# One weight split moved from the end of the attention loop to the end of the head projections

## The reference, cut to what matters

```
qkv = (h @ w_qkv).reshape(B, S, 3, N_DIL, N_HEADS, HEAD_DIM)      # layer A: 3 groups; layer B: 1 group
q, k = rope(rmsnorm(q)), rope(rmsnorm(k))
scores = q @ k.T * scale;  scores = where(mask, scores, -inf)
p = exp(scores - max);  o = p @ v / sum(p)
x = x + attn @ w_o;  x = x + conv_ffn(rmsnorm(x))
```

## Time and profile before

| what | value |
|---|---|
| median of 3 runs | 1137.72 us |
| lowest and highest | 1136.93 and 1138.73 us |
| time of the profiled execution | 1137.72 us |
| its span (first to last instruction) | 1135.9 us, so 1.8 us lie around it |
| mean granted clock of PE | 0.992 |
| attention of `half_a0` and `half_a1`, first transpose | at 452.2 and at 583.5 us |
| attention of `half_b0` and `half_b1`, first transpose | at 858.3 and at 908.3 us |

### The profile page before, as it was taken

The page is one execution under the profiler, slowest core; times in us unless marked ns, Lnnn a source line. Parts: engine busy times, 40 slices in busy tenths (PEclk is TensorE's granted clock), DMA queues, the critical chain, the costliest instruction groups (busy, mean ns, idle before and its releaser), DMA issues.

```text
span 1135.9 us, 19220 instructions
## 1 busy us (share of the span) xinstructions
PE 1115.0 (98%) x7046; PEld 974.4 (86%) x7046; DVE 790.6 (70%) x1439; ACT 641.0 (56%) x1086; POOL 13.3 (1%) x23
## 2 busy tenths in 40 slices
PE   9998899999999999999999999999999999999998
PEld 7876789989987888888888999999887779999997
DVE  5867656555557667477675787787885757877876
ACT  5465455454456556565564665555666556655554
POOL 0000100000000000000000000000000000000000
PEclk9998899999999999999999999999999999999999
DMA  9552145666646565055622466556552624665562
GB/s 322 164 181 75 56 131 186 186 186 190 190 136 199 172 188 164 20 188 165 203 95 92 133 195 211 185 170 200 168 174 87 196 89 142 186 207 192 160 207 103
DMA packets 117037, 184.34 MB, mean 162 GB/s; under 512 B 6640, under 2 KB 70384, under 8 KB 116720
## 3 DMA queue, kind: packets, MB, share of 16 engines
q1 hardware_dynamic: 116688, 183.23, 51.1%
q10 hardware_dynamic: 288, 0.29, 0.1%
HBM read 182.45 MB, written 1.05 MB: 162 GB/s over the span
## 4 chain that ended last, share of the span: by engine, by line
PE 89%; DVE 4%; ACT 3%; issue 2%; DMA 1%; SPq 0%; DVEq 0%; ACTq 0%
PE ps L679 10%; PE ps L655 10%; PE ps L681 10%; PE ps L680 10%; PE ps L657 10%; PE ps L656 10%; PE ps L739 5%; PE ps L738 5%; PE ps L740 5%; PE ps L815 2%; PE ps L832 2%; PE ps L797 2%; PE ps L858 1%; ACT w_hi L1132 1%; DVE w_lo L1649 1%
## 5 line engine op out<-in xcount | busy, mean ns | idle before, releaser
L1649 DVE TENSOR_TENSOR w_lo<-w_stage,w_hi 128x1024 fp32r<-128x1024 f32 x336 | 403.6, 1221 | 191.8 <-ACT w_hi L1132 190.9
L1132 ACT ACTIVATE w_hi<-w_stage 128x1024 fp32r<-128x1024 f32 x336 | 349.4, 1054 | 202.1 <-PE ps L657 106.4
L679 PE MATMUL ps<-aT_hi,w_hi 128*128 128x256 f32 x992 | 281.5, 284 | 1.2 <-DVE aT_lo L1663 1.1
L681 PE MATMUL ps<-aT_hi,w_lo 128*128 128x256 f32 x992 | 280.7, 283 | 0.0
L680 PE MATMUL ps<-aT_lo,w_hi 128*128 128x256 f32 x992 | 280.7, 283 | 0.0
L655 PE MATMUL ps<-w_hi,aT_hi 128*128 128x512 f32 x480 | 191.7, 399 | 3.7 <-issue 2.2
L679 PEld LDWEIGHTS ps<-aT_hi,w_hi 128*128 128x128 f32 x992 | 190.2, 192 | 2.8 <-issue 1.3
L680 PEld LDWEIGHTS ps<-aT_lo,w_hi 128*128 128x128 f32 x992 | 190.3, 192 | 1.1
L681 PEld LDWEIGHTS ps<-aT_hi,w_lo 128*128 128x128 f32 x992 | 190.3, 192 | 0.0
L657 PE MATMUL ps<-w_hi,aT_lo 128*128 128x512 f32 x480 | 187.7, 391 | 0.0
L656 PE MATMUL ps<-w_lo,aT_hi 128*128 128x512 f32 x480 | 187.5, 391 | 0.0
(11 more groups left out here) (226 smaller groups left out, 1178.8 us busy)
## 6 DMA issues: line engine op xcount, KB each, us to landing
w_stage<-in_ffn_w_up SPq DMA_DIRECT2D x88, 512.0 KB, 4.7
w_stage<-in_a_w_qkv SPq DMA_DIRECT2D x72, 512.0 KB, 3.7
w_stage<-in_ffn_w_down SPq DMA_DIRECT2D x44, 512.0 KB, 3.5
w_stage<-in_w_up SPq DMA_DIRECT2D x32, 512.0 KB, 3.7
w_stage<-in_w_down SPq DMA_DIRECT2D x32, 512.0 KB, 4.1
w_stage<-in_w_in SPq DMA_DIRECT2D x24, 512.0 KB, 4.8
w_stage<-in_b_w_qkv SPq DMA_DIRECT2D x24, 512.0 KB, 4.3
w_stage<-in_w_out SPq DMA_DIRECT2D x8, 512.0 KB, 3.6
```

Of the source, the lines that this page charges most:

```text
L679: pe.matmul(o, wh, aT_hi[:, k, :], start=(k == 0), stop=False)
L681: last = pe.matmul(o, wl, aT_hi[:, k, :], start=False, stop=(k == KT - 1))
L1132: act.activation(w_hi[:, slot, :], w_in[:, slot, :], ACT.Copy).then_inc(hi_done[slot], 1)
L1649: dve.tensor_tensor(w_lo[:, slot, :], w_in[:, slot, :], w_hi[:, slot, :].bitcast(F32), ALU.subtract).then_inc(lo_done[slot], 1)
```

## The change: what it does

In both instruction lists, ACT's and DVE's, the split of the last quarter of a half (`12 * NG - 1` = 35 in layer A, 11 in layer B, both the same as `q0 + 11` of the last group) leaves step u = 7 of `attention` and becomes the last thing in `project_heads`. On ACT it then stands behind the move of `v{g}0`, on DVE behind the move of `v{g}1`, both ahead of the first step of the loop. This happens in all four halves. No instruction is added or removed, and PE, POOL and SP keep their lists.

```
@@ ACT @@
-            def attention(stg, units, last):
+            def attention(stg, units):
...
                         act.activation(turned_ring[v % 2][:, 0, 0:W], ps[:, b, 0:W], ACT.Copy).then_inc(drained[b], 1)
-                    if u == n - 1:
-                        split(stg, last)
                     if u + 1 < n:
                         exps(stg, units[u + 1], u + 1)
...
                         exps(S_, units[1], 1)
                         evac_v(S_, f"v{g}0", i, vv[:, 0, g * 512:(g + 1) * 512], stat("rtok", 2)[:, 0:1])
+                        split(S_, q0 + 11)
                     else:
...
@@ DVE @@
-            def attention(stg, units, last):
+            def attention(stg, units):
...
                         dve.tensor_copy(turned_ring[v % 2][:, 1, 0:W], ps[:, b, 0:W]).then_inc(drained[b], 1)
-                    if u == n - 1:
-                        split(stg, last)
                     if u >= 3 and u % 2:
...
                 dve.tensor_scalar(vv[:, 1, (groups - 1) * 512:groups * 512], ps[:, b, :], stat("rtok", 2)[:, 1:2], None,
                                   ALU.mult).then_inc(drained[b], 1)
+                split(S_, q0 + 11)
...
-                attention(S_, units, 12 * NG - 1)
+                attention(S_, units)
...
-                attention(S_, units, 11)
+                attention(S_, units)
```

## The result

The changed kernel takes 1146.76 us (median of 4 runs, 1146.54 to 1147.61) against 1137.95 us for the kernel before (1136.93 to 1138.73; 4 runs). The ratio is 1.0080, its 95% interval [1.0063, 1.0096]. The forecast was 1143.9: right in direction, but the change costs 8.8 us, not 6.2.

What follows compares the result with a forecast made beforehand. PE, busy 98% of the span, was taken to bound the kernel. 2 x 1.49 in A plus 2 x 1.62 in B gave 6.2 us over 1137.72, so 1143.9 us; 8-in-10 range 1141.3 to 1147.0.

Steps and rivals of the forecast that it cites:

- Nothing gained at u = 7: Old place of the split: freeing it gains 0, bounded by 0.28 us in each half of B, 0.6 in all.
- ACT's part costs 0: Head of the loop, layer A: ACT copies head A 0.1 us later, covered by PE's scores of unit 3; cost 0.
- DVE's queue in A, 1.49 us: Layer A, loop head: split and maxima delay DVE's copy emptying bank 5; PE's head B of unit 1 waits 1.49 us.
- Layer B, 1.62: Layer B, loop head: same DVE list, shorter instructions; PE's head B of unit 1 waits 1.62 us per half.
- Paid once per half, no second wait: Behind the stall: exponentials of unit 2 and DVE's next head B copy come in time, so no further delay.
- the 1.4 to 1.7 named: Sign in the trace: one PE idle stretch of 1.4 to 1.7 us per loop, inside unit 1's transposes.
- The load 19 us earlier, 0 us: Load of quarter 7 of the next stage: issued at about 454.3 instead of 473.5, meeting no traffic; 0 us.
- So I leave the clock at full: Four added PE gaps of about 1.5 us, with dense products ahead of them: clock expected to stay full.
- The fall: Rival, chance 0.10: clock drops to 1.2 GHz behind a gap, 3.0 us each; one gives 1146.9, two 1149.9.
- the gap at 94 us: First block: PE gap of 1.36 us before 94.58, small products on both sides, ahead of a mean clock of 0.63.
- the 1.23 us idle at 126 us: Stretch cited for a full clock: PE idle 1.23 of 4.00 us, dense products ahead, clock 1.00.
- 0.56 us to spare: Layer A before: bank 5 copy over at 454.22, PE wanted it at 454.78; basis of rival "partly hidden", chance 0.11.

Runs made afterwards that it cites:

- The filled kernels: Changed kernel, and kernel with the split moved in layer B alone, each plus 10 extra PE products at the stall at u = 2: 1144.85 and 1142.63 us.

## Why the prediction was off, step by step

- **Nothing gained at u = 7: right.** Behind u = 8 the next projection begins at 478.13 in the changed kernel and at 474.44 before; the 3.69 us are the 2.13 and 1.56 from earlier, and nothing came back.
- **ACT's part costs 0: right**, by the kernel with DVE's half behind the copy: 0.0 us in A, and in B the wait that is left is for DVE.
- **DVE's queue in A, 1.49 us: right to the instruction, 0.08 short.** Head B restarts at 458.39 - 2.13 = 456.26; the forecast was 456.27. But the four transposes behind the restart take 458.98 - 458.39 = 0.59 us where I had half of 1.02. Measured 1.57 per half.
- **Layer B, 1.62: 0.05 to 0.07 short**, by the same term. Measured 1.67 to 1.69 where the clock stayed at full.
- **Paid once per half, no second wait: right**, and the shift was constant through the MLPs (0.02 to 0.08 us). Idle time shown for PE is 1.34 us, under the 1.4 to 1.7 named, since the row's 0.66 us of the products before it run into the gap.
- **The load 19 us earlier, 0 us: right.** It was issued at 456.48, so at 454.35 without the 2.13 us.
- **"So I leave the clock at full" is the step that failed.** The fall was a rival with a chance of 0.10 and one price, 3.0 us. In layer B it is the usual case: of the 12 runs with only B changed, two took 1140.0 and 1142.4 us, at mean clocks of 0.993 and 0.991, and the other ten 1144.7 to 1147.8, at 0.985 to 0.988. (Only two of the ten were profiled, each with a fall in both loops; for the rest it is read from time and mean clock.) The price of one fall was 1.5 or 2.8 us. My reason was that dense products stand ahead of this change's gaps and small ones ahead of the gap at 94 us. Neither holds. In the profiles of B the dense projection had ended 2.4 us before the stall, and PE had already waited at the first transposes there. And ahead of the gap at 94 us dense products run too, until 92.35 us, 0.9 us before it; only then come small groups:

```profile
91.96 0.39 PE L657 MATMUL ps<-w_hi,aT_lo 128*128 128x512 f32 x1
...
92.72 0.49 PE L921 MATMUL ps<-kT,qT 64*128 64x128 f32 x4
```

  The stretch that spoke for a full clock, the 1.23 us idle at 126 us, is a filled one: right ahead of its transposes stand 26 `spin` instructions, of the sort that took the falls away in B.

```profile
121.28 3.63 PE L866 MATMUL ps<-consts 128*128 128x128 f32 x26
```

  The Trainium skill, whose rule I had set beside it ("TensorE: Matmul & The Clock Gate", part 1), says that the gate follows how busy PE has been recently. The filled kernels agree with it: 3.8 us less for the same waits.
- The sum as it stands: 2 x 1.57 + 2 x 1.69 = 6.5 us of stalls (fastest execution of the changed kernel 1144.16, where the forecast was 1143.9), 0.3 more than forecast, and some 2.3 us of the 8.8 between the medians that are left for the clock, in the loops of B and in the first block; how they divide was not measured beyond the one profile (1.48 and 2.13). That the median of 1146.76 comes near the 1146.9 that the rival gave for one fall is luck: the one fall in a loop of that profile cost half of the rival's 3.0 us, and the first block made up the rest.
- **The 2.13 us in the first block** are no effect of the edit that could be shown: the same changed kernel, profiled again, stood at -0.09 us there. In that block, with small products and waits, the clock falls in every profile, each time at other points, for 17 to 27 us in all. The kernel before had 17 us of it at the lower level in its profile, the changed one 24 in its first and 17 in its second. The four profiles with 24 us or more, each of another kernel, were late by 1.8 to 2.1 us there against the profile of the kernel before; the other nine stood between -0.6 and +0.9. The runs of the kernel before alone spread from 1136.9 to 1140.8. That all six executions of the changed kernel at the first measurement were above 1146.5, at mean clocks of 0.988 and 0.989, while later ones reached 1144.2 is left open.

## What to carry to other kernels

Before an instruction moves, write down what stands behind it in its engine's list at the new place and when the bottleneck wants the first of those; a share of idle time over the loop says nothing about that step. Here a split of 1.2 us delayed a 0.7 us copy by 2.0 us, because it also had to wait for the other engine's half, and 0.56 us to spare could not hold that. And price a new gap in PE's work twice, once as a wait and once as a possible fall of the clock at it. In this kernel the price of the second was 1.5 to 2.8 us, about as much as the wait or more; a gap of the same length in A, between larger groups, never had to pay it.

## What the runs showed of the hardware that was not expected

In layer B, a loop whose products come in groups of 0.4 to 0.7 us, PE's idle stretch of 1.35 us came with a fall of the clock in five of the eight such stretches that were profiled unfilled, and in most executions by their times. Each fall lasted 3.4 or 6.8 us at 1.2 GHz and cost 1.5 or 2.8 us. It began between 0.1 us before PE was busy again and 2.0 us after it, so it can show on products that run without a stop. Ten instructions of 0.12 us that compute nothing, put into the stretch, left the wait itself as it was, and the clock stayed at full in the loops of both filled kernels' profiles. Their runs spread by 1.2 and 2.2 us, those of the unfilled ones beside them and of the first with B alone by 5.3 to 6.4; the changed kernel's six at the first measurement by 1.4. So useless work in a short wait of PE can make a kernel faster: 3.8 us here.
